# Latent attention unrolled over its head pairs, with the next pair's queries and the last head's values placed among scores and transposes

## What is computed

```python
def mla_attention(c_q, c_kv, k_pe, cos, sin, q_norm_g, w_uq, kv_norm_g, w_ukv):
    q = (rms_norm(c_q, q_norm_g) @ w_uq).reshape(B, S, 8, 128 + 64)
    q_nope, q_pe = q[..., :128], apply_rope(q[..., 128:], cos, sin)
    kv = (rms_norm(c_kv, kv_norm_g) @ w_ukv).reshape(B, S, 8, 128 + 128)
    k_nope, v = kv[..., :128], kv[..., 128:]
    k_rot = apply_rope(k_pe, cos, sin)               # one rotary key for all heads
    s = einsum(q_nope, k_nope) + einsum(q_pe, k_rot) # per head, 512 x 512
    p = softmax(s * 192 ** -0.5)
    return einsum(p, v)                              # 512 x 1024
```

## Time and profile before

| | us |
|---|---|
| three runs | 3279.91, 3292.45, 3298.45 |
| median | 3292.45 |
| profiled execution, span | 3293.5 |
| PE busy / DVE busy / ACT busy in it | 3119.8 / 2073.9 / 367.9 |
| attention with its value products, first to last (478.58 to 703.54) | 224.96 |

### The profile page before, as it was taken

How to read it: one execution, slowest core, us unless ns; L and a number is a source line. 1 busy time by engine, 2 the same in 40 slices (tenths; PEclk the granted TensorE clock), 3 DMA queues, 4 the chain that set the end, 5 groups by cost and what they waited for, 6 DMA issues and landing times.

```text
span 3293.5 us, 27033 instructions
## 1 busy us (share of the span) xinstructions
PE 3119.8 (95%) x10342; PEld 1889.4 (57%) x10342; DVE 2073.9 (63%) x2874; ACT 367.9 (11%) x653; POOL 682.0 (21%) x557
## 2 busy tenths in 40 slices
PE   8999998899999898999989999999999999999797
PEld 5444443334445577678874447884458853478443
DVE  5356532342668779889997766656566666656675
ACT  1233212320101211112210000000000000000000
POOL 0000000000021134322222333222222333223240
PEclk9999999999999999999999999999999999999899
DMA  6222221047797678998998999999999999999985
GB/s 267 77 77 70 86 65 44 10 166 261 294 408 309 258 316 358 417 387 305 350 350 350 389 422 421 421 415 417 421 421 421 419 419 416 422 421 421 412 368 233
DMA packets 152515, 1029.69 MB, mean 313 GB/s; under 512 B 16464, under 2 KB 21712, under 8 KB 35664
## 3 DMA queue, kind: packets, MB, share of 16 engines
q0 software_dynamic: 78512, 557.88, 41.6%
q1 hardware_dynamic: 73888, 470.24, 36.4%
HBM read 1007.08 MB, written 20.97 MB: 312 GB/s over the span
## 4 chain that ended last, share of the span: by engine, by line
DMA 41%; PE 33%; DVE 18%; issue 4%; ACT 2%; POOL 2%; DVEq 0%; SPq 0%; ACTq 0%; POOLq 0%
DMA arena<-peer_v,arena 40%; PE ps L693 10%; DVE arena L1750 7%; PE ps L1077 4%; PE ps L845 3%; DVE arena L1788 2%; DVE arena L1739 2%; PE ps L935 2%; PE ps L863 2%; PE ps L770 1%; PE ps L1050 1%; PE ps L799 1%; ACT arena L1117 1%; POOL arena L611 1%; PE ps L785 1%
## 5 line engine op out<-in xcount | busy, mean ns | idle before, releaser
L1077 PE MATMUL ps<-arena 128*128 128x512 f32 x2048 | 884.8, 595 | 52.8 <-DVE arena L1800 52.0
L1050 PE MATMUL ps<-arena 128*128 128x256 f32 x4096 | 898.3, 381 | 9.6 <-ACT arena L1333 8.9
L1050 PEld LDWEIGHTS ps<-arena 128*128 128x128 f32 x4096 | 778.7, 191 | 118.9 <-ACT arena L1333 9.7
L1750 DVE SCALAR_TENSOR_TENSOR arena<-arena 128x2048 f32<-128x2048 f32 x256 | 601.8, 2351 | 298.8 <-DMA arena<-peer_v,arena 233.1
L1739 DVE CUSTOM_DVE_ANT_0 arena<-arena 128x2048 f32<-128x2048 f32 x256 | 586.2, 2290 | 288.4 <-DMA arena<-peer_u,arena 286.8
L1077 PEld LDWEIGHTS ps<-arena 128*128 128x128 f32 x2048 | 390.6, 191 | 544.8 <-issue 490.6
L611 POOL DMA_INDIRECT arena<-peer_u,arena x256 | 346.8, 1354 | 1108.3 <-DVE arena L1739 909.3
L622 POOL DMA_INDIRECT arena<-peer_v,arena x256 | 309.2, 1208 | 755.0 <-DVE arena L1750 725.8
L693 PE MATMUL ps<-arena 128*128 128x512 f32 x800 | 345.2, 592 | 1.1 <-ACT arena L1117 1.1
L693 PEld LDWEIGHTS ps<-arena 128*128 128x128 f32 x800 | 151.9, 190 | 192.2 <-issue 192.2
L1117 ACT ACTIVATE arena<-ps 128x512 f32<-128x512 f32 (+3 forms) x247 | 145.2, 611 | 774.9 <-PE ps L855 138.8
(11 more groups left out here) (179 smaller groups left out, 1804.9 us busy)
## 6 DMA issues: line engine op xcount, KB each, us to landing
arena<-peer_ut SPq DMA_DIRECT2D x128, 1024.0 KB
arena<-peer_vt SPq DMA_DIRECT2D x128, 1024.0 KB
arena<-w_row SPq DMA_DIRECT2D x52, 1024.0 KB
arena<-w_mix SPq DMA_DIRECT2D x48, 1024.0 KB
arena<-w_once SPq DMA_DIRECT2D x74, 512.0 KB, 3.5
arena<-w_feat SPq DMA_DIRECT2D x20, 1024.0 KB
dense_gates<-arena SPq DMA_DIRECT2D x8, 2048.0 KB, 7.3
arena<-dense_gates POOLq DMA_DIRECT2D x11, 1024.0 KB, 24.2
```

The source lines that it names most:

```text
L1050: last = pe.matmul(ps[:, (e // 2) % 4, (e % 2) * DT:(e % 2 + 1) * DT], w[:, kt * P:(kt + 1) * P], XTD[:, kt * DT:(kt + 1) * DT], start=(kt ...
L1077: last = pe.matmul(bank(4 + (c % 2) * 2 + tb), G[:, t * DT + tb * P:t * DT + (tb + 1) * P], w[:, i * 512:(i + 1) * 512], start=(t == 0), s ...
L1750: dve.scalar_tensor_tensor(out=acc, in0=VB[e], scalar=AV[r // 4 % 2][:, r % 4:r % 4 + 1], in1=acc, op0=ALU.mult, op1=ALU.add).then_inc(v_f ...
```

## The change

- The loop over pairs is unrolled, and step m = 8 hp + n counts over all pairs. `scores(0)` of the next pair follows step 7 directly.
- The three query products of the next pair are placed after steps 3, 4 and 7; those of the first pair around the value products (V), which go to banks 4 to 7.
- Values of a pair's second head are placed in step 2 of the next pair, those of the first head in step 6. They read V directly; the copies VH and their wait are gone. Both use bank 2.
- Scores use banks 3, 4, 5 in turn (before: four banks).
- The rotary queries go to two buffers QZ, one for each head, zero in the other head's 64 partitions, so that both products of a score have 128 rows. DVE's rotation is cut in pieces among steps 4, 5, 6 and 0.
- On DVE the probabilities of step m follow the maximum of step m.
- In the last pair ACT's squares and DVE's sums of finished heads are placed among the steps; the last two transposes and the last head's values stand among the first output products, and the sum over features in the second of them.

```diff
-SCORE_BANKS = [4, 5, 2, 3]
+PAIRS = HEADS // 2
+OUT_BANK = 2
+def score_bank(m):
+    return 3 + m % 3
+def turn_bank(m):
+    return 6 + m % 2
+def query_bank(hp, k):
+    return (3 * hp + k) % 2
...
         WQ = place("wq", 1536)
-        at0[0] += 512
+        QZ = [place("rotary query of even heads", S)]
         QN = [place(f"qn{e}", S) for e in range(2)]
-        QR = place("qr", S)
+        QC = place("query times cos", S)
         PM = [place(f"pm{e}", S) for e in range(4)]
         PT = place("pt", 4 * S)
-        VH = [place(f"vh{e}", 4 * P) for e in range(2)]
-        assert at0[0] == MISC
+        QZ.append(place("rotary query of odd heads", S))
+        assert at0[0] <= MISC
         UB = [place("u0", D, 8192), place("u1", D, 10240), place("u2", D, SC2)]
...
-            pool.wait_ge(kv_ev, 16)
-
-            def copy_v(hp):
-                for e in range(2):
-                    pool.wait_ge(pv_mm, hp * 2 + (e + 1))
-                    pool.sem_inc(pool_tick, 1)
-                    pool.tensor_copy(VH[e].rearrange("p (t v) -> p t v", t=4),
-                                     V.rearrange("p (t w) -> p t w", t=4)[:, :, bass.ds(hp * 256 + e * P, P)]
-                                     ).then_inc(vh_done, 1)
-
-            with pool.Fori(0, HEADS // 2 - 1) as hp:
-                copy_v(hp)
...
-            copy_v(HEADS // 2 - 1)
+            for e in range(2):
+                pool.memset(QZ[e], 0.0).then_inc(qz_set, 1)
+            for hp in range(1, PAIRS):
+                pool.wait_ge(qn_mm, 2 * hp)
+                pool.dma_start(WQ, wq_pairs[hp]).then_inc(wq_full, 16)
             pool.wait_ge(qn_mm, HEADS)
             pool.dma_start(GAIN_G, gains[4:5, :].partition_broadcast(P)).then_inc(gain2_in, 16)
             pool.dma_start(GAIN_B, gains[5:6, :].partition_broadcast(P)).then_inc(gain2_in, 16)
-            pool.wait_ge(pv_mm, HEADS + 2)
+            pool.wait_ge(pv_mm, HEADS)
             pool.dma_start(GAIN1_G, gains[2:3, :].partition_broadcast(P)).then_inc(gain1_in, 16)
...
+            def query(hp, k):
+                part = (2, 0, 1)[k]
+                if k == 0:
+                    pe.wait_ge(wq_full, 16 * (hp + 1))
+                    if hp:
+                        pe.wait_ge(qn_ev, 2 * hp - 1)
+                elif k == 1:
+                    if hp:
+                        pe.wait_ge(qn_ev, 2 * hp)
+                else:
+                    pe.wait_ge(qpe_read, hp + 1)
+                for i in range(4):
+                    last = pe.matmul(bank(query_bank(hp, k)), WQ[:, part * 512 + i * P:part * 512 + (i + 1) * P],
+                                     C[:, (4 + i) * S:(5 + i) * S], start=(i == 0), stop=(i == 3))
+                last.then_inc(qn_mm if k else qpe_mm, 1)
...
+            query(0, 0)
+            query(0, 1)
+            pe.wait_ge(kv_ev, 8)
+            all_values(0, t)
+            query(0, 2)
+            pe.wait_ge(kv_ev, 12)
+            all_values(1, t + 2)
+            t += 4
...
+            def scores(m):
+                hp, n = m // 8, m % 8
+                e, qb = n // 4, n % 4
+                if m == 1 or m == 2:
+                    pe.wait_ge(kv_ev, 12 + m)
+                if m >= 3:
+                    pe.wait_ge(exp_done, m - 2)
+                if n % 4 == 0:
+                    pe.wait_ge(qr_done, 2 * hp + e + 1)
+                    pe.wait_ge(qn_ev, 2 * hp + e + 1)
+                to = bank(score_bank(m))
+                pe.matmul(to, QN[e][:, qb * P:(qb + 1) * P], KN[:, (2 * hp + e) * S:(2 * hp + e + 1) * S],
+                          start=True, stop=False)
+                pe.matmul(to, QZ[e][:, qb * P:(qb + 1) * P], KR, start=False, stop=True).then_inc(s_mm, 1)
+            def turn(m):
+                pe.wait_ge(p_done, m + 1)
+                if m < 2:
+                    pe.wait_ge(kv_ev, 15 + m)
+                else:
+                    pe.wait_ge(pt_ev, m - 1)
+                for k in range(4):
+                    last = pe.transpose(ps[:, turn_bank(m), k * P:(k + 1) * P], PM[m % 4][:, k * P:(k + 1) * P], IDENT)
+                last.then_inc(t_mm, 1)
+            def values(hp, e):
+                h = 2 * hp + e
+                pe.wait_ge(pt_ev, 4 * h + 4)
+                if h:
+                    pe.wait_ge(o_ev, h)
+                for k in range(4):
+                    last = pe.matmul(bank(OUT_BANK), V[:, k * 1024 + h * P:k * 1024 + (h + 1) * P],
+                                     PT[:, k * S:(k + 1) * S], start=(k == 0), stop=(k == 3))
+                last.then_inc(pv_mm, 1)
+            for hp in range(PAIRS):
+                for n in range(8):
+                    m = 8 * hp + n
+                    scores(m)
+                    if n == 2 and hp:
+                        values(hp - 1, 1)
+                    if n == 6:
+                        values(hp, 0)
+                    if m >= 2:
+                        turn(m - 2)
+                    if hp + 1 < PAIRS and n in (3, 4, 7):
+                        query(hp + 1, (3, 4, 7).index(n))
...
-            pe.wait_ge(o_ev, HEADS + 2)
-            for h in range(2):
-                if h:
-                    pe.wait_ge(rms_done, 4)
-                for c in QUAD:
-                    if h == 0 and c == 1:
-                        sum_over_features(4, 7)
-                    mix([0], [c], 2 * h, 2, f"mix0.{h}.{c}")
+            last_m = 8 * PAIRS - 1
+            turn(last_m - 1)
+            mix([0], [0], 0, 1, "mix0.0.0")
+            turn(last_m)
+            mix([0], [0], 1, 1, "mix0.0.0")
+            values(PAIRS - 1, 1)
+            mix([0], [1], 0, 1, "mix0.0.1")
+            sum_over_features(4, 7)
+            mix([0], [1], 1, 1, "mix0.0.1")
+            pe.wait_ge(o_ev, HEADS)
+            for c in (2, 3):
+                mix([0], [c], 0, 2, f"mix0.0.{c}")
+            pe.wait_ge(rms_done, 4)
+            for c in QUAD:
+                mix([0], [c], 2, 2, f"mix0.1.{c}")
...
+            def query(hp, e):
+                act.wait_ge(qn_mm, 2 * hp + e + 1)
+                evict(QN[e], bank(query_bank(hp, e + 1))).then_inc(qn_ev, 1)
...
+            def exp(m):
+                act.wait_ge(nmx_done, m + 1)
+                if m >= 4:
+                    act.wait_ge(t_mm, m - 3)
+                act.activation(PM[m % 4], bank(score_bank(m)), ACT.Exp, bias=NM2[m % 4], scale=ATT_SCALE,
+                               accum_out=RSM2[m % 4]).then_inc(exp_done, 1)
+            def turned(m):
+                act.wait_ge(t_mm, m + 1)
+                qb = m % 4
+                evict(PT.rearrange("p (k s) -> p k s", k=4)[:, :, qb * P:(qb + 1) * P],
+                      bank(turn_bank(m)).rearrange("p (k s) -> p k s", k=4)).then_inc(pt_ev, 1)
+            def output(hp, e):
+                act.wait_ge(pv_mm, 2 * hp + e + 1)
+                evict(feature(2 * hp + e), by_block(bank(OUT_BANK))).then_inc(o_ev, 1)
+            def attention_square(k):
+                act.wait_ge(o_ev, k + 1)
+                square(16 + k, feature(k))
+            for hp in range(PAIRS):
+                for n in range(8):
+                    m = 8 * hp + n
+                    if hp and n == 0:
+                        query(hp, 1)
+                    if hp + 1 < PAIRS and n == 5:
+                        query(hp + 1, 0)
+                    exp(m)
+                    if n == 2 and hp:
+                        output(hp - 1, 1)
                     if n == 6:
-                        output(0)
-                    turned(n - 2)
-                turned(6)
-                turned(7)
-                output(1)
-            act.wait_ge(o_ev, HEADS + 2)
-            squares(16, 8, [feature(k) for k in range(8)])
+                        output(hp, 0)
+                    if m >= 2:
+                        turned(m - 2)
+                    if hp == PAIRS - 1 and n >= 3:
+                        attention_square(n - 3)
+            turned(8 * PAIRS - 2)
+            attention_square(5)
+            turned(8 * PAIRS - 1)
+            attention_square(6)
+            output(PAIRS - 1, 1)
+            attention_square(7)
...
+            def rotate_first(hp):
                 dve.wait_ge(qpe_mm, hp + 1)
+                src = bank(query_bank(hp, 0))
+                dve.tensor_tensor(QC, src, COS, ALU.mult)
+                for k in range(2):
+                    swapped_part(src, k)
+            def rotate_second(hp):
+                src = bank(query_bank(hp, 0))
+                swapped_part(src, 2)
+                link(swapped_part(src, 3))
+                dve.sem_inc(qpe_read, 1)
+            def rotated(e):
+                here = slice(e * ROPE, (e + 1) * ROPE)
+                dve.tensor_tensor(QZ[e][here, :], QC[here, :], TMP[here, :], ALU.add).then_inc(qr_done, 1)
+            def row_max(m):
+                dve.wait_ge(s_mm, m + 1)
+                link(dve.tensor_reduce(MX2[m % 4], bank(score_bank(m)), AX, ALU.max))
```

(54 more changed lines are left out.)

110 lines of the change are left out of this document (6 added, 104 removed).

## The result

| | us |
|---|---|
| changed kernel, median of 4 | 3250.33 (3249.71 to 3251.81) |
| kernel before on the same chip, median of 4 | 3292.09 (3279.91 to 3298.45) |
| ratio | 0.9876, interval 0.9856 to 0.9896 |
| predicted | 3240, range 3224 to 3264 |

A forecast was written before the change was run, and what follows sets the result against it. Attention was taken as bound by in-order TensorE. New stage 166.7 + 0.8 + 2 x 0.5 + 2.0 + 1.8 = 172.3 against 224.96 saves 52.7; 3293.5 - 52.7 = 3240.8, forecast 3240, range 3224 to 3264 (own range 3228 to 3252).

The forecast's parts named there:

- two rivals that did not happen (3251 and 3253): Attention: 128 rows save nothing, 3251, chance 0.05; the clock still falls at every values run, 3253, chance 0.12.
- Idle of 26.1: Attention stage: PE's idle time before the change, 26.1 us, counted among the 58.3 the change can reach.
- The walk through the queues: Attention's new order followed step by step: PE waits only before values, 0.8 in pair 0, 0.5 each in pairs 1 and 2, 2.0 in the last.
- 128 rows: Score products in attention: rotary products over all 128 rows, zeros in the other head's half, save 10.5 us; bounds 0 and 10.5.
- the price by the pace: Score products: each 128-row record priced at 0.429 us, a pair 1.72 against 2.10 or 2.01 with 64 rows, saving 10.5.
- The rival that they save nothing: Score products: the pace is set by the change of operands, not of rows; 10.5 us lost, 3251, chance 0.05.
- Clock: Attention: records at the low clock cost 16.6 us before; the granted clock would be 1.00 in nearly all of the new stage.
- the 28.7 that I gave as a sign: Values products in attention, L799's successor: busy near 28.7 us in the profile after, not 41.3.
- The one low run that I charged behind the 1.7 gap: Last pair's values products in attention: one run at the low clock behind a wait of 1.7, charged 1.8 us.
- rms_done: Output products after attention: rms_scale's 16.1 us stays hidden by 2, so the second half has no wait for rms_done.
- A microsecond saved on PE here is a microsecond of the end: Attention stage: all that follows waits for its result, so the whole saving of 52.7 us reaches the end.
- My rival was named for it: Stages after attention: the saving is given back downstream; full give-back 3293, half 3266, chance 0.08 for half or more.

The follow-up runs named there:

- late_sums: Changed kernel with ScalarE's squares and VectorE's sums of attention's features after all steps, as before the change: 3254.53 us.
- half_rows: Changed kernel with the rotary product of each score on 64 rows again, all else as changed: 3255.64 us.
- only_rows: Kernel before with only the two zero-padded QZ buffers, so rotary products have 128 rows; loops, order and copies as before: 3277.81 us, ratio 0.9959.
- delay_65: Changed kernel with 65 further unread products on TensorE before the second half of the first output products: 3303.12 us.
- delay_8: Changed kernel with 8 further unread products (6.9 us) on TensorE before the second half of the first output products: 3248.19 us.

## Why the prediction was right, and what of it was not

The sum against the profile: 3240.8 predicted; less 3.2, since the stage gave 55.9 and not 52.7; and 11.3 for the rest: 3248.9, the span. With 1.8 around it, the time.

That 3250 lies in the range is in part luck. The stage was read rightly in the main. Then a term of 11.3 that the sum put at nothing moved the time close to the upper edge of the forecast's own range, 3252; of it, 3.2 were hidden by a stage that gave more than forecast. And the time came out where two rivals that did not happen (3251 and 3253) had their prices. The total alone could not tell them apart; the stretches do.

- *Idle of 26.1*: right. I left 3.8 for the new kernel, it has 2.9. The walk through the queues gave 0.34 and 1.7 before values where 0.28 and 1.68 came; the 0.8 that it gave for pair 0 did not come. late_sums shows the cause of most of the 1.68.
- *128 rows*: they save, as the price by the pace said, but 7.4 net in this program, where half_rows was expected at 11; in the old one about 10. The rival that they save nothing falls with half_rows. The rule that the prediction set beside that rival, the Trainium skill's that a weight load costs by its columns and not by its rows ("TensorE: Matmul & The Clock Gate", "LDWEIGHTS (loading the stationary operand)"), agrees with the trace: in half_rows the loads of L799 take 185 ns with 64 rows and those of L797 191 with 128. It just doesn't set the pace of the products. I missed that transposes beside 128-row products are quicker as well: a group takes 634.46 - 634.03 = 0.43, not 0.49, 1.8 in all.
- *Clock*: the 16.6 went, all of it. Which part of the change did that is only bounded: the unrolled order alone keeps the clock up with 64 rows (half_rows), and only_rows lost 10.2 of it with the gaps left in. L817 is at 29.5 and not at the 28.7 that I gave as a sign, but by the tails of its runs (3.70 each, not 3.6), at full pace. The one low run that I charged behind the 1.7 gap did not come; the windows over the gap and over the values behind it stand at 1.00:

```profile
632.00:638.00 6.00, 4.34 (x17) 2.03 (x15) 3.71 (x10) 3.68 (x10) 0.00 (x0) 1.00 0.00 1
638.03:641.57 3.54, 3.54 (x9) 1.58 (x10) 2.16 (x6) 1.24 (x3) 0.00 (x0) 1.00 0.02 5
```

  That and transposes that stay at full clock in every bare step are also what this case has to say on the Trainium skill's sentence that transposes don't count as busy ("TensorE: Matmul & The Clock Gate", Part 4): it may hold, but a fifth of the time in a step (0.43 of 2.15) did no harm here.
- *rms_done*: hidden, as forecast; PE has no wait between 659.63 and 717.99.
- *"A microsecond saved on PE here is a microsecond of the end"*: this is the step that failed, by 11.3 of 55.9 in the profiles, 14 by the first medians and 12 by the medians of all runs. The sum has no term for it. My rival was named for it and had 0.08, but for a half or more; about a fifth came back. One of the prediction's own signs of being wrong showed it too: the stretch from the sum over features to the end, 2582.3 before, grew, to 2590.0 (3248.8 - 658.77).

What the runs show in its place: the rest does not shorten or lengthen with how early it starts (delay_65). In the profiles three waits of PE for VectorE or for an eviction behind it grew, by 4.8 in the first window and by 6.1 in the fourth, the two longest of them with VectorE behind gathers. Records that last longer, at the lower granted clock, add 4.9; other waits got shorter, so that 11.3 is the sum. A part comes and goes: the same program, shifted by 0, 7, 28 and 56 us, has rests that differ by up to 9 without order. A part goes with the old program, whose rest is the shortest in both its profiles and by the medians, shifted or not; only_rows, with one part of the change in it, lies between. What in the program does that stays open; code, where the gains' loads fall and the state of the DMA queues weren't separated.

## What to carry to other kernels

Follow an in-order queue step by step with durations from the trace, lookahead and all: here it gave the two sorts of waits that came to a tenth of a microsecond, and one of 0.8 that didn't come. Do not carry the whole saving over a later stage in which another resource is full: here part of it was lost there, in waits that come or don't. Put a term of some microseconds on it, and judge small edits upstream by their own stretch and not by the total. The 64-row products cost time at both neighbours here, so where zeros can fill the other half for nothing, try it.

## What the runs showed of the hardware that was not expected

- The granted clock goes neither by the last gap alone nor by the rows. In only_rows values ran low three times of four behind a gap of 0.69 and never behind 1.83. In the unrolled programs gaps of 1.68 and 2.02 before values left the clock up. With 64-row products and gaps it fell at seven of eight values runs (before), with 128-row products and nearly the same gaps at three (only_rows), with 64-row products and a single gap of 0.8 at none (half_rows). The same V products behind the same gap of 2.15 ran low in all three profiles of the old order with 64 rows, and not in only_rows.
- A 64-row product slows what stands beside it: a group of transposes takes 0.49 there and 0.43 beside 128-row products, and a pair of products 2.01 and 1.72.
- 6.9 us of further work on PE (delay_8) left the time unchanged within 2.2, and the kernel before spreads over 25 us with a stage that repeats to 0.1 us over three profiles, so the spread should lie in the rest.
- That spread goes with the mean granted clock, which is on record for 41 of the 45 runs: the 11 runs at 0.985 and above took 3279 to 3289, the 12 at 0.981 and below 3290 to 3304. An estimate from these numbers: from 0.987 to 0.980 some 46 us more of the span are at the lower of the two levels, 1.2 and not 2.4 GHz, and busy all through them PE would lose 23, nearly the whole spread. Whether the clock makes the waits of a slower run or follows them isn't shown; in the rows above it is low right behind them.
